# Two rings of six slots for streamed weights, splits three slots ahead in the experts, and tokens fetched from two halves and then turned

## The reference, cut to what matters

```python
def moe_swiglu(h, router_w, router_b, w_gate, w_up, w_down):
    t = h.reshape(B * S, Dm)                              # 256 tokens x 1024
    logits = (t @ router_w) + router_b                    # 8 experts
    top_vals, top_idx = lax.top_k(logits, 2)
    gates = jax.nn.softmax(top_vals, axis=-1)
    combine = sum(one_hot(top_idx, 8) * gates[..., None])
    for e in range(8):                                    # hidden width 1408
        out = out + combine[:, e:e + 1] * swiglu(t, w_gate[e], w_up[e], w_down[e])
```

## Time and profile before

| | us |
|---|---|
| median of 3 runs (1519.66 to 1522.49) | 1520.29 |
| the profiled execution | 1521.61 |
| its span, first to last instruction | 1519.9 |
| mean granted TensorE clock | 0.989 |
| PE / DVE / ACT busy, share of the span | 96% / 80% / 59% |

### The profile page before, as it was taken

The page is one execution under the profiler, slowest core; times in us unless marked ns, Lnnn a source line. Parts: engine busy times, 40 slices in busy tenths (PEclk is TensorE's granted clock), DMA queues, the critical chain, the costliest instruction groups (busy, mean ns, idle before and its releaser), DMA issues.

```text
span 1519.9 us, 19672 instructions
## 1 busy us (share of the span) xinstructions
PE 1457.8 (96%) x7256; PEld 1193.7 (79%) x7257; DVE 1221.4 (80%) x1662; ACT 894.2 (59%) x1191; POOL 5.6 (0%) x18
## 2 busy tenths in 40 slices
PE   6999999999999999999999999979999999999996
PEld 5888888887788887777788887857788788878875
DVE  6767879767758889778878787696788888898997
ACT  6656664546565664566533433556777677777765
POOL 0000000000000000000000000000000000000000
PEclk9999999999999999999999999979999999999998
DMA  9653457874444448553577686313498888888892
GB/s 355 248 214 146 174 185 257 310 291 166 167 170 190 153 181 319 225 204 118 194 270 276 236 294 226 139 56 111 143 347 313 327 336 303 332 314 335 323 326 99
DMA packets 53421, 356.14 MB, mean 234 GB/s; under 512 B 6096, under 2 KB 7120, under 8 KB 12896
## 3 DMA queue, kind: packets, MB, share of 16 engines
q1 hardware_dynamic: 52592, 352.15, 62.3%
q0 software_dynamic: 320, 2.65, 0.5%
q10 hardware_dynamic: 432, 0.30, 0.1%
HBM read 354.03 MB, written 1.05 MB: 234 GB/s over the span
## 4 chain that ended last, share of the span: by engine, by line
PE 71%; DVE 18%; ACT 6%; issue 4%; DMA 1%; DVEq 0%; SPq 0%; ACTq 0%
PE ps L435 21%; PE ps L437 21%; PE ps L436 21%; DVE wlo L1646 7%; ACT whi L1110 2%; PE ps L600 1%; PE ps L527 1%; PE ps L651 1%; DVE acc L1672 1%; PE ps L676 1%; DVE tok L1897 1%; ACT attn_scratch L1296 1%; DMA raw<-stream_dram 1%; DVE tok L2391 1%; PE ps L705 1%
## 5 line engine op out<-in xcount | busy, mean ns | idle before, releaser
L1646 DVE TENSOR_TENSOR wlo<-raw,whi 128x2048 fp32r<-128x2048 f32 (+2 forms) x302 | 648.3, 2164 | 104.9 <-ACT whi L1110 91.3
L1110 ACT ACTIVATE whi<-raw 128x2048 fp32r<-128x2048 f32 (+2 forms) x302 | 543.5, 1815 | 242.2 <-PE ps L437 239.1
L435 PE MATMUL ps<-whi,xhi 128*128 128x512 f32 (+3 forms) x1360 | 534.0, 393 | 14.3 <-DVE wlo L1646 4.7
L437 PE MATMUL ps<-whi,xlo 128*128 128x512 f32 (+3 forms) x1360 | 522.3, 384 | 0.0
L436 PE MATMUL ps<-wlo,xhi 128*128 128x512 f32 (+3 forms) x1360 | 521.5, 383 | 0.0
L435 PEld LDWEIGHTS ps<-whi,xhi 128*128 128x128 f32 x1360 | 256.9, 189 | 74.8 <-issue 8.9
L437 PEld LDWEIGHTS ps<-whi,xlo 128*128 128x128 f32 x1360 | 256.8, 189 | 51.3
L436 PEld LDWEIGHTS ps<-wlo,xhi 128*128 128x128 f32 x1360 | 257.3, 189 | 46.1
L435 PE MATMUL ps<-whi,ahi 128*128 128x512 f32 x440 | 177.8, 404 | 3.5 <-DVE wlo L1646 2.9
L436 PE MATMUL ps<-wlo,ahi 128*128 128x512 f32 x440 | 174.2, 396 | 0.0
L437 PE MATMUL ps<-whi,alo 128*128 128x512 f32 x440 | 174.2, 396 | 0.0
(11 more groups left out here) (310 smaller groups left out, 1133.5 us busy)
## 6 DMA issues: line engine op xcount, KB each, us to landing
raw<-stream_dram SPq DMA_DIRECT2D x315, 1024.0 KB, 5.3
raw<-stream_dram SPq DMA_DIRECT2D x32, 512.0 KB, 4.9
attn_scratch<-toep_dram POOLq DMA_DIRECT2D x1, 2048.0 KB, 9.3
raw<-stream_dram SPq DMA_DIRECT2D x2, 528.0 KB, 5.2
h<-x_dram SPq DMA_DIRECT2D x2, 512.0 KB, 4.6
y<-tok SPq DMA_DIRECT2D x4, 256.0 KB, 2.5
head_scratch<-w_s_dram SPq DMA_DIRECT2D x1, 512.0 KB, 13.5
head_scratch<-vg_dram SPq DMA_DIRECT2D x1, 512.0 KB, 10.9
```

The source lines that it names most:

```text
L435: pe.matmul(o, xh, wh, start=start, stop=False)
L437: return pe.matmul(o, xl, wh, start=False, stop=stop)
L1110: act.activation(whi[:, q % SPL, 0:w], raw[:, s % RAW, 0:w], ACT.Copy).then_inc(sem("hi_done"), 1)
L1646: dve.tensor_tensor(wlo[:, q % SPL, 0:w], raw[:, s % RAW, 0:w], whi[:, q % SPL, 0:w].bitcast(F32), ALU.subtract).then_inc(sem("lo_done"), 1)
```

## The change

`wlo` no longer has memory of its own: it is laid over `raw` (same address, six slots), and DVE writes each low half in place of the slot that it came from (`low(q)`). What that frees goes to `whi`, which has six slots too. A load now waits until PE is done with the slot six before it (`w_used`); only behind a modulation slot it still waits for `lo_done`. In the dense layers the splits keep their distance (LEAD = 3 stands where SPL = 3 stood, AHEAD stays 2); in the experts it is MORE = 3 instead of AHEAD = 2, and the fixed 3 and 4 become 4 and 5.

The tokens are fetched differently. ACT writes the normed tokens as `thi` in fp32r, DVE their rest `tlo`, before it waits for the ranks. `gather` makes, for each of two halves of the features, four matmuls of 512 columns, `G` (now fp32r) stationary and the tokens moving. ACT copies the result to SBUF (`copy_gathered`), and PE turns it back with 8 transposes (`turn_gathered`), which stand after the first of the down slots; the rest follows as before. `xg`, `abx`, `G` and the new tiles lie at other places.

```diff
-SPL = 3
+SPL = 6
+LEAD = 3
 AHEAD = 2
+MORE = 3
+        def low(q):
+            return wlo[:, PL.s_of[q] % RAW, :]
+        with nc.sbuf_tensor("wlo", [P, RAW, SLOT], F32R) as wlo:
+            pass
         raw = sb("raw", [P, RAW, SLOT])
         whi = sb("whi", [P, SPL, SLOT], F32R)
-        wlo = sb("wlo", [P, SPL, SLOT], F32R)
...
+        thi = alo[:, FE // P:FE // P + 8, :].rearrange("p (t k) s -> p t (k s)", t=NT)
+        tlo = ahi[:, FE // P + 1:FE // P + 9, :].rearrange("p (t k) s -> p t (k s)", t=NT)
...
             def load(s, i=None, src=None):
                 if s >= RAW:
-                    sp.wait_ge(sem("lo_done"), s - RAW + 1 if i is None else i * EXP + (s - RAW + 1))
+                    if PL.kind[s - RAW] == "a":
+                        sp.wait_ge(sem("lo_done"), s - RAW + 1)
+                    else:
+                        done = PL.q[s - RAW] + 1
+                        sp.wait_ge(sem("w_used"), done if i is None else i * EXP + done)
...
-            pe.wait_ge(sem("tokens"), NT)
+            pe.wait_ge(sem("tokens_split"), NT)
             def gather():
                 pe.wait_ge(sem("places"), T.up("x_g"))
                 pe.wait_ge(sem("g_taken"), T("x_g"))
                 for b in range(2):
+                    c = slice(b * W, (b + 1) * W)
+                    for t in range(NT):
+                        pe.matmul(ps[:, 5 + 2 * b, :], G[:, t, :], thi[:, t, c], start=t == 0, stop=False)
+                        m = pe.matmul(ps[:, 5 + 2 * b, :], G[:, t, :], tlo[:, t, c], start=False, stop=t == NT - 1)
+                    m.then_inc(sem("g_psum"), 1)
+
+            def turn_gathered():
+                for b in range(2):
+                    pe.wait_ge(sem("xt_copied"), T.up("x_xt"))
                     for k in range(4):
-                        for t in range(NT):
-                            m = pe.matmul(ps[:, 5 + 2 * b, k * P:(k + 1) * P], TA[:, t, (4 * b + k) * P:(4 * b + k + 1) * P],
-                                          G[:, t, :], start=t == 0, stop=t == NT - 1)
-                    m.then_inc(sem("g_psum"), 1)
+                        m = pe.transpose(ps[:, 5 + 2 * b, k * P:(k + 1) * P], xt[:, (4 * b + k) * P:(4 * b + k + 1) * P], ident[:, :])
+                    m.then_inc(sem("g_turned"), 1)
...
-            def out_of(i, first=False):
+            def out_of(i, first=False, turn_next=False):
                 for j in range(6):
+                    if j == 1 and turn_next:
+                        turn_gathered()
                     if j == 2:
                         turn(5)
...
             for t in range(NT):
-                act.activation(TA[:, t, :], h[:, t, :], ACT.Copy, scale=st[:, 6 + t:7 + t]).then_inc(sem("tokens"), 1)
-            split(used[0] + AHEAD)
+                act.activation(thi[:, t, :], h[:, t, :], ACT.Copy, scale=st[:, 6 + t:7 + t]).then_inc(sem("tokens"), 1)
+            split(used[0] + MORE)
             act.wait_ge(sem("g2"), 1)
...
+            def copy_gathered():
+                for b in range(2):
+                    act.wait_ge(sem("g_psum"), T.up("x_gp"))
+                    act.activation(xt[:, b * W:(b + 1) * W], ps[:, 5 + 2 * b, :], ACT.Copy).then_inc(sem("xt_copied"), 1)
...
                 used[0] += 2
-                split(used[0] + AHEAD, i, EXP)
+                split(used[0] + MORE, i, EXP)
...
                 if not last:
-                    split(used[0] + 3, i, EXP)
-                    take_gathered(lambda: split(used[0] + 4, i, EXP))
+                    copy_gathered()
+                    split(used[0] + MORE + 1, i, EXP)
+                    take_gathered(lambda: split(used[0] + MORE + 2, i, EXP))
...
-                    dve.tensor_tensor(wlo[:, q % SPL, 0:w], raw[:, s % RAW, 0:w], whi[:, q % SPL, 0:w].bitcast(F32),
+                    dve.tensor_tensor(low(q)[:, 0:w], raw[:, s % RAW, 0:w], whi[:, q % SPL, 0:w].bitcast(F32),
                                       ALU.subtract).then_inc(sem("lo_done"), 1)
...
             dve.tensor_tensor(g2[:, :, 0], mx8[:, :, 1], mx8[:, :, 0], ALU.subtract).then_inc(sem("g2"), 1)
+            for t in range(NT):
+                dve.wait_ge(sem("tokens"), t + 1)
+                dve.scalar_tensor_tensor(tlo[:, t, :], h[:, t, :], st[:, 6 + t:7 + t], thi[:, t, :].bitcast(F32), ALU.mult, ALU.subtract)\
+                    .then_inc(sem("tokens_split"), 1)
             dve.wait_ge(sem("ranks"), 1)
...
-            split(used[0] + AHEAD)
+            split(used[0] + MORE)
             split_gathered()
```

More of the change, by code:

```diff
@@ L455, in product @@
                     wh = whi[:, q % SPL, 0:n * width].rearrange("p (k n) -> p k n", k=n)
-                    wl = wlo[:, q % SPL, 0:n * width].rearrange("p (k n) -> p k n", k=n)
+                    wl = low(q)[:, 0:n * width].rearrange("p (k n) -> p k n", k=n)
                     for t in range(NT):
@@ L569, in normed_product @@
                         wh = whi[:, q % SPL, :].rearrange("p (k n) -> p k n", k=4)
-                        wl = wlo[:, q % SPL, :].rearrange("p (k n) -> p k n", k=4)
+                        wl = low(q).rearrange("p (k n) -> p k n", k=4)
                         for k in range(4):
@@ L998, in hidden @@
                     wh = whi[:, s % SPL, 0:4 * w].rearrange("p (k n) -> p k n", k=4)
-                    wl = wlo[:, s % SPL, 0:4 * w].rearrange("p (k n) -> p k n", k=4)
+                    wl = low(s)[:, 0:4 * w].rearrange("p (k n) -> p k n", k=4)
                     for k in range(4):
@@ L1029, in out_of @@
                             m = mm3(ps[:, 3 + n, :], ahi[:, k, 0:P], alo[:, k, 0:P], whi[:, s % SPL, a:a + W],
-                                    wlo[:, s % SPL, a:a + W], k == 0, k == FE // P - 1)
+                                    low(s)[:, a:a + W], k == 0, k == FE // P - 1)
                     m.then_inc(sem("w_used"), 1)
@@ L1048, in expert @@
                     gather()
-                out_of(i, first)
+                out_of(i, first, turn_next=not last)
             gather()
+            turn_gathered()
             expert(0, first=True)
             with pe.Fori(0, NE - 2) as i:
-                T.loop(i, x_acc=6, x_tr=6, x_g=1, x_y=1, x_a=6, x_s=2, x_gt=1)
+                T.loop(i, x_acc=6, x_tr=6, x_g=1, x_xt=2, x_y=1, x_a=6, x_s=2, x_gt=1)
                 expert(i)
@@ L1082, in _ @@
                         pe.drain()
-                        for name, k in (("g_psum", 2), ("x_tr", 6), ("gt_psum", 1), ("w_used", EXP), ("y_psum", 2)):
+                        for name, k in (("g_psum", 2), ("g_turned", 2), ("x_tr", 6), ("gt_psum", 1), ("w_used", EXP), ("y_psum", 2)):
                             pe.sem_inc(sem(name), k)
@@ L1270, in conv_ffn @@
                     evac()
-                    convolve(j, (lambda: split(used[0] + SPL)) if j == n - 2 else lambda: None)
-                split(used[0] + SPL + 1)
-                convolve(n - 1, lambda: split(used[0] + SPL + 2))
+                    convolve(j, (lambda: split(used[0] + LEAD)) if j == n - 2 else lambda: None)
+                split(used[0] + LEAD + 1)
+                convolve(n - 1, lambda: split(used[0] + LEAD + 2))
             def evac_gated(m):
@@ L1331, in attention @@
                         copy(i - 2)
-                split(used[0] + SPL)
+                split(used[0] + LEAD)
                 hi(3)
@@ L1562, in expert @@
                 if not last:
-                    split(used[0] + 3, i, EXP)
-                    take_gathered(lambda: split(used[0] + 4, i, EXP))
+                    copy_gathered()
+                    split(used[0] + MORE + 1, i, EXP)
+                    take_gathered(lambda: split(used[0] + MORE + 2, i, EXP))
                 else:
-                    split(used[0] + 4, i, EXP)
+                    split(used[0] + MORE + 2, i, EXP)
                 hi_of(5)
@@ L1600, in _ @@
                         act.drain()
-                        for name, k in (("xg", 2), ("hi_done", EXP), ("x_silu", 6), ("gt_copied", 1), ("x_hi", 6), ("yg_hi", 2)):
+                        for name, k in (("xt_copied", 2), ("xg", 2), ("hi_done", EXP), ("x_silu", 6), ("gt_copied", 1), ("x_hi", 6), ("yg_hi", 2)):
                             act.sem_inc(sem(name), k)
```

29 lines of the change are left out of this document (15 added, 14 removed).

## The result

| | before | after |
|---|---|---|
| median of 5 runs each, us | 1520.6 | 1512.85 |
| lowest to highest | 1519.66 to 1523.17 | 1511.35 to 1515.0 |
| profiled execution, its span | 1521.61, 1519.9 | 1511.35, 1509.6 |
| mean granted clock | 0.989 | 0.988 |

The ratio of the runs is 0.9946 (95%: 0.9936 to 0.9957): 0.54% faster, at the predicted time (1512.7). The total was right, and so were several terms; two of its reasons were not, as the experiments show. The median before differs a little from the one ahead of the prediction, since it is over five runs here and over three there.

The account below looks back on a forecast made before the run. PE was taken to bound the kernel, 96% busy, with DVE next. Terms -5.4 - 5.0 - 2.9 + 4.1 + 1.6 = -7.6 gave 1514.0 us profiled, 1512.7 median; range 1508 to 1517, 8 in 10 for 1508 to 1521.

Parts of the forecast that it names:

- The fetch: Token fetch between experts: products plus transposes take 2.73 us instead of 3.5, saving 0.77; seven fetches give -5.4 us.
- The new wait in the turn: PE's wait for ACT's two copies before turning tokens: 0.4 to 1.0 us each, hidden with 1.8 us to spare.
- The stops: PE's two waits for low halves per expert vanish: 0.7 us in six middle experts, 0.8 in the first, -5.0 us.
- Three slots ahead: Experts' splits one slot further ahead spread DVE's disturbances over 2.8 us more, so both PE stops go: -5.0 us.
- D: Rival: the middle experts' stops come from DVE's order and remain, 1517.7 us; chance 0.16 together with another rival.
- The start: Before the first expert: ACT's extra split and DVE's extra low half lengthen the chain 4.1 us; clock fall adds 1.6.
- The gather's chain: Before the first expert: places, fetch, copies, turn and scaling end about 1082.5, covered with 1.6 us spare; no saving there.
- The rule on transposes and the clock: At the start's hole, transposes do not count for the clock as products do; +1.6 us stands, otherwise perhaps nothing.
- The last expert: Last expert's PE stop shortens by 1.3 us and the clock stays up, 1.6 us: together -2.9, second low half 0.7 late.
- Loads later at no cost: Loads released by PE need 9.5 us of 14 in the experts' hidden part, leaving 4.5 for queues: cost nothing.
- Rival B: Loads come too late in the experts, 2.2 us lost eight times, +17.6 us, 1530 us in all; chance 0.12.
- rival A: DVE takes over as bound, the middle experts' period stays 53.35 us, sum +1.3, 1521.6 us, no change; chance 0.12.

Follow-up runs that it names:

- the last column: Two kernels with six high slots and splits three ahead: old fetch 1519.14 us (middle expert 52.38), new fetch, the kernel after, 1512.85 us (51.60).
- rings and old fetch: Kernel before with low halves in place, six high slots, loads released by PE, and experts' splits three ahead, fetch unchanged: 1519.14 us, ratio 0.9987.
- other start: Kernel after with Exp ahead of ACT's second split and the tokens' low half ahead of DVE's second weight low half: 1510.44 us, ratio 0.9926.
- the rings alone: Kernel before with low halves in place, six high slots and loads released by PE; old fetch, splits two ahead: 1515.06 us, ratio 0.9966.
- three edits: Kernel after with reordered start, 8 and 8 unused products in PE's start stops, and the last expert's low half ahead of the sum: 1508.97 us, ratio 0.9921.
- without fillers: The kernel with three edits, minus the extra products whose results nobody uses in PE's stops at the start: 1508.73 us, ratio 0.9918.

## Why the prediction was right, and where it was not

**The fetch: right,** 0.77 predicted, 0.78 between the two kernels of the last column. By the slots' ends it is 0.87, hence the 6.1 in the table. What I missed is the condition: I added the term as if it stood by itself, but with splits two ahead the same fetch makes an expert 0.65 to 0.76 longer. The 5.4 us belong to fetch and distance together.

**The new wait in the turn: right.** The copies take 0.60 (predicted 0.4 to 1.0); PE's waits in the middle experts hold none for them.

**The stops: near in size (0.7 predicted, 0.97 an expert measured), wrong in the main cause.** The step that failed is in "Three slots ahead", which gave the whole gain to the one slot more in hand, over which DVE's disturbances "are spread over a further 2.8 us". I had named the ring ("no longer held back by PE") in half a sentence; it gives 0.60 of the 0.97, and three high slots take exactly that back. The distance gives 0.37 with the old fetch. The two reasons stood in one term, so that the total came out near was partly luck. Of my rivals, D said that the distance might not be the cause, but put the other cause in DVE's order, where the high ring was the answer. The earlier trace rows had it: 9.4 us an expert of ACT waiting for PE's release, against the 3.4 that DVE waited for ACT.

**The start: right.** +4.1 predicted, 4.0 measured with the old and with the new fetch, and the clock 2.0 for 1.6. The first of its two falls, at 1073.66, was not foreseen; it slowed the fetch, which was covered. The gather's chain was indeed covered: with three ahead, the new fetch adds 0.1 us to the start; with two ahead, where nothing covers it, it adds 3.4 to the end of the first expert's first slot. The rule on transposes and the clock that the prediction weighed (the Trainium skill, TensorE: Matmul & The Clock Gate, Part 4) stays untested: the clock was at 1.00 while the first transposes ran and at 0.50 from 1080.5, but PE was idle after them, so the fall needs no rule about transposes.

**The last expert: right,** -2.9 predicted, -2.7 measured, with the second low half late by 0.8 (predicted 0.7).

**Loads later at no cost: the step that failed.** "It fits with 4.5 us for queues on ACT and DVE" counted from a load's release to PE's use. But the split stands ahead of the operations on earlier slots, which PE is still working on: on ACT ahead of their Silu, on DVE ahead of their multiplication. These have no 4.5 us. One slot (about 2.8 us) later costs 25 us. The kernel after sits on that edge: the profiled execution paid 1.3 us once, where the prediction had nothing. Rival B's price (17.6 us) and sign were wrong for this change. That loads come late was there; what PE waits for was not the slot itself. (By its own terms rival A's sum is +1.4, not +1.3, which changes nothing.)

**The total** agrees better than its parts: stops 2.2 us better, a late load 1.3 and the end 0.8 worse, the rest within 0.7 each, and in the medians little or no gain from the dense layers.

## What to carry to other kernels

When an engine waits for a ring's release, lengthen that ring first and alone: here three more slots gave 5 us, and the edits around it only mattered after it. A shorter step in front of a queue that is just in time turns into a wait unless the work is also started earlier, so time such edits in pairs. Count a load's margin on every engine that touches it, to the first instruction that stands behind its wait in that engine's order, not only to the engine that uses the data.

## What was not expected of the hardware

Two of the kernels with splits three ahead spread widely: 1512.75 to 1523.91 (rings and old fetch, twelve runs), 1503.88 to 1514.54 (other start, six runs), while the rings alone lie within 1.9 us. It is no rule for the distance: the kernels with three edits, with and without fillers, also split three ahead and lie within 2.2 us. The profiles show late-load stops at changing experts, the same code waiting in one and not in another; what makes a load late in one expert was not tried. Low halves written over their own source run at 2.29 us for 2048 elements, as before (2.29).
